# Two blocks on one core: the head of the first block with x transposed on the host, unscaled x for q, k, v and four gates, and idle TensorE products

## The reference, cut to what matters

```
xn   = rms_norm(x, mix_norm)                       # over the 1024 columns of a row
proj = xn @ w_in + b_in                            # 1024 x 4352
q, k, v, cb, cc, cx, ga, gc = split(proj)          # 512, 128, 128, 512, 512, 512, 1024, 1024
attn = sliding_window_attention(q, k, v, sinks)
conv = cb * causal_depthwise_conv(cc * cx, conv_w)
merged = sigmoid(ga) * (attn @ w_attn_branch) + sigmoid(gc) * (conv @ w_conv_branch)
h = x + merged @ w_out
```

## Time and profile before

| what | value |
|---|---|
| runs | 1231.47 us median of 3 (1231.33 to 1234.18) |
| the profiled execution's own time | 1231.15 us |
| its span, first to last instruction | 1229.4 us |
| TensorE products (PE) | 1206.5 us busy, 98%, 5844 instructions |
| TensorE weight loads (PEld) | 1013.6 us |
| VectorE (DVE), ScalarE (ACT), GpSimd (POOL) | 830.3, 554.4, 343.1 us |
| HBM read | 112.25 MB |

### The profile page before, as it was taken

How to read it: one execution, slowest core, us unless ns; L and a number is a source line. 1 busy time by engine, 2 the same in 40 slices (tenths; PEclk the granted TensorE clock), 3 DMA queues, 4 the chain that set the end, 5 groups by cost and what they waited for, 6 DMA issues and landing times.

```text
span 1229.4 us, 15053 instructions
## 1 busy us (share of the span) xinstructions
PE 1206.5 (98%) x5844; PEld 1013.6 (82%) x5844; DVE 830.3 (68%) x1532; ACT 554.4 (45%) x965; POOL 343.1 (28%) x267
## 2 busy tenths in 40 slices
PE   7999999999999999999999999999999999999997
PEld 6888888888888888888887789888788889888886
DVE  6788434436788536653568966778966766778964
ACT  6667332324444314433434456644335555553433
POOL 0255499972000000000003853343003033342000
PEclk9999999999999999999999999999999999999999
DMA  5322232223323322332323233222222332322221
GB/s 197 105 69 69 95 103 94 94 86 103 96 93 104 102 88 90 96 116 91 99 65 109 99 109 99 90 89 77 77 70 91 116 103 87 92 86 88 76 71 69
DMA packets 36152, 115.33 MB, mean 94 GB/s; under 512 B 3824, under 2 KB 6384, under 8 KB 36080
## 3 DMA queue, kind: packets, MB, share of 16 engines
q1 hardware_dynamic: 36080, 114.36, 29.3%
HBM read 112.25 MB, written 2.10 MB: 93 GB/s over the span
## 4 chain that ended last, share of the span: by engine, by line
PE 76%; DVE 14%; ACT 6%; issue 2%; POOL 1%; DMA 0%; SPq 0%; ACTq 0%
PE ps L273 73%; DVE RA L250 6%; DVE FA L250 4%; ACT RA L242 3%; DVE FA L262 2%; ACT FA L247 1%; ACT RA L246 1%; POOL FA L250 1%; DVE FA L1267 1%; PE ps L1301 1%; DVE RA L262 1%; DVE FA L1271 1%; PE ps L747 0%; DMA FA<-x 0%; ACT FA L246 0%
## 5 line engine op out<-in xcount | busy, mean ns | idle before, releaser
L273 PE MATMUL ps<-RA 128*128 128x512 f32 (+3 forms) x5460 | 1177.3, 376 | 7.1 <-DVE RA L250 4.8
L273 PEld LDWEIGHTS ps<-RA 128*128 128x128 f32 x5460 | 970.8, 188 | 191.1 <-DVE RA L250 4.9
L250 DVE TENSOR_TENSOR RA<-FA,RA 128x1024 fp32r<-128x1024 f32 (+4 forms) x316 | 329.3, 1051 | 185.6 <-ACT RA L242 183.6
L242 ACT ACTIVATE RA<-FA 128x1024 fp32r<-128x1024 f32 (+6 forms) x336 | 278.8, 858 | 334.7 <-PE ps L273 164.5
L250 POOL TENSOR_TENSOR FA<-FA 128x512 f32<-128x512 f32 (+1 forms) x89 | 122.1, 1372 | 550.5 <-ACT FA L246 451.5
L266 POOL TENSOR_SCALAR FA<-FA 128x256 f32<-128x256 f32 (+2 forms) x117 | 141.7, 1222 | 190.4 <-DVE FA L270 189.3
L262 DVE SCALAR_TENSOR_TENSOR FA<-ps,FA 128x512 f32<-128x512 f32 (+3 forms) x137 | 98.1, 721 | 95.6 <-PE ps L273 50.3
L247 ACT ACTIVATE FA<-FA 128x512 f32<-128x512 f32 (+3 forms) x113 | 61.0, 541 | 99.1 <-DVE FA L1271 78.4
L246 ACT ACTIVATE FA<-ps,FA 128x512 f32<-128x512 f32 x61 | 41.6, 685 | 123.5 <-PE ps L273 123.5
L262 DVE SCALAR_TENSOR_TENSOR FA<-FA 128x4 f32<-128x4 f32 (+4 forms) x166 | 81.8, 501 | 17.8 <-ACT FA L246 6.6
L250 DVE TENSOR_TENSOR RA<-ps,RA 128x256 fp32r<-128x256 f32 (+3 forms) x111 | 54.7, 529 | 21.4 <-ACT RA L246 18.9
(11 more groups left out here) (46 smaller groups left out, 305.8 us busy)
## 6 DMA issues: line engine op xcount, KB each, us to landing
FA<-w_units SPq DMA_DIRECT2D x190, 512.0 KB, 3.5
FA<-rel SPq DMA_DIRECT2D x16, 256.0 KB, 3.3
FA<-w_units SPq DMA_DIRECT2D x8, 384.0 KB, 3.0
FA<-x SPq DMA_DIRECT2D x4, 512.0 KB, 6.8
FA<-dmat SPq DMA_DIRECT2D x8, 256.0 KB, 3.2
out<-FA SPq DMA_DIRECT2D x8, 256.0 KB, 2.2
FA<-gain SPq DMA_DIRECT2D x1, 512.0 KB, 3.7
FA<-positions SPq DMA_DIRECT2D x1, 256.0 KB, 3.5
```

Of the source, the lines that this page charges most:

```text
L242: return lambda eng: eng.activation(dst, src, ACT.Copy)
L250: return lambda eng: eng.tensor_tensor(dst, a, b, op)
L273: return lambda e: e.matmul(dst, a, b, start=start, stop=stop_)
```

## The change

x comes twice from the host: transposed, as eight tiles of 128 x 512 (256 KB each), and by rows. The transposed tiles are loaded straight to where they are kept; the 32 transposes, the copies from PSUM and the loads in four pieces are gone. The row form is loaded in four pieces of 512 KB, only for the sums of squares; the first two stand behind all x tiles on SyncE's queue, the last two behind the fourth weight unit. The loads of `pvec` and `ident` move from SyncE's queue to ScalarE's. The first weight unit comes in two halves, and `gemm_first` runs its products in another order: for each half, four of high x high, four of high x low, four of low x high. Ahead of them stand ten products of a zeroed tile with itself, whose result nobody reads (`WARM`).

Unscaled x has a place of its own (X0H, X0L), so normalised x no longer overwrites it. The units k and v, and four gate units (ga0, gc0, ga1, gc1), which move up from the loop over the mixing units to here, run on unscaled x; VectorE multiplies their results by r, and the four gates' tanh then runs on SBUF. r is wanted later: its spread moves from the middle of q.w1 to the middle of q.w3, and the normalising of the eight tiles is spread over the evacuations of k, v and the four gates. The loop over the mixing units runs its six remaining gate pairs two ahead, with four buffers per gate; its last two turns have no gates.

```diff
+WARM = 10
...
-F_COLS = Y + 6760
-XIN, JUNK = Y, Y + 4096
+XIN = Y
+QT = Y + 256
+TG = Y + 6760
+F_COLS = TG + 2048
+X0H, X0L = Z + 16896, Z + 20992
...
+    for m in range(2):
+        u += [(f"ga{m}", tall("w_in", 2304 + 128 * m)), (f"gc{m}", tall("w_in", 3328 + 128 * m))]
     for t in range(4):
         u.append((f"cc{t}", tall("w_in", 1280 + 128 * t)))
         u.append((f"cx{t}", tall("w_in", 1792 + 128 * t)))
         u.append((f"cb{t}", tall("w_in", 768 + 128 * t)))
     for m in range(8):
-        u.append((f"ga{m}", tall("w_in", 2304 + 128 * m)))
-        u.append((f"gc{m}", tall("w_in", 3328 + 128 * m)))
+        if m < 6:
+            u.append((f"ga{m + 2}", tall("w_in", 2304 + 128 * (m + 2))))
+            u.append((f"gc{m + 2}", tall("w_in", 3328 + 128 * (m + 2))))
...
+        def gemm_first(key, banks, xh, xl):
+
+            h, l = w_slot[0]
+            for i in range(2):
+                halves = ((h, xh, [f"xh.{i}", f"wh.0.{i}"]), (h, xl, [f"xl.{i}"]), (l, xh, [f"wl.0.{i}"]))
+                for n, (w, xop, after) in enumerate(halves):
+                    for m, b in enumerate(banks):
+                        fin = f"gemm.{key}" if i == 1 and n == 2 and m == 3 else None
+                        T(fin, after if m == 0 else [], mmul(bank(b), R(w + 512 * i + 128 * m, 128), R(xop(i)),
+                                                             i == 0 and n == 0, False))
...
-        dma("ident", [], F(ID, 128), consts[0], "c0")
...
-
-            dma(f"x.{j}", [], steps(F(XIN + 256 * j, 256), [[1024, 4], [1, 256]]),
-                x_cols[:, :, 256 * j:256 * j + 256], f"x{j}")
...
-        load_x(0)
-        dma("pvec", [], F(PV, PV_COLS), pvec, "c1")
-        load_to(0)
-        load_x(1)
-        load_to(1)
+        def load_x(k):
+
+            dma(f"x.{k}", [], F(H + 512 * k), x[k], f"x{k}")
+
+        def load_half(i):
+
+            dma(f"raw.0.{i}", [], F(RAW + 512 * i), w_units[0][:, 512 * i:512 * i + 512], f"rawfirst{i}")
+
+        def load_rows(t):
+
+            dma(f"rows.{t}", [], F(XIN + 1024 * t, 1024), x_rows[128 * t:128 * t + 128], f"rows{t}")
+
+        dma("pvec", [], F(PV, PV_COLS), pvec, "c1", "scalar")
+        dma("ident", [], F(ID, 128), consts[0], "c0", "scalar")
+        for i in range(2):
+            load_x(i)
+            load_half(i)
+        issued[0] = 1
         load_x(2)
         load_x(3)
+        load_to(1)
+        load_x(4)
+        load_x(5)
         load_to(2)
+        load_x(6)
+        load_x(7)
+        for t in range(2):
+            load_rows(t)
         HB, NSINK, SS, MS, RC, TMP = columns(16), columns(8), columns(4), columns(4), columns(4), columns(4)
-        SQ = columns(8)
...
-        def turn_x(k):
-            for t in range(4):
-                b = xt_bank(k)
-                T(f"xT.{k}" if t == 3 else None, [f"x.{k // 2}", "ident"] + take(f"bank{b}") if t == 0 else [],
-                  lambda e, t=t, b=b: e.transpose(bank(b, 128, 128 * t), F(XIN + 1024 * t + 128 * k, 128), F(ID, 128)))
+        x0h = lambda k: X0H + 512 * k
+        x0l = lambda k: X0L + 512 * k
+
+        for n in range(WARM):
+            T(None, ["z1a"] if n == 0 else [], mmul(bank(7), R(K2A, 128), R(K2A), True, True))
...
-            b, gain = xt_bank(k), F(PV + PV_G1 + k, 1)
-            A(f"xh.{k}", [f"xT.{k}", "pvec"], func(R(xh(k)), bank(b), ACT.Copy, scale=gain))
-            yield
-            V(f"xl.{k}", [f"xh.{k}"], stt(R(xl(k)), bank(b), gain, Rf(xh(k)), ALU.mult, ALU.subtract))
...
-        def keep_x(k):
-            b = xt_bank(k)
-            (V if k < 4 else A)(f"h0.{k}", [f"xl.{k}"], (lambda e: e.tensor_copy(F(H + 512 * k), bank(b))) if k < 4 else copy(F(H + 512 * k), bank(b)))
-            free(f"bank{b}", f"h0.{k}")
...
-        def square_x(half):
-            for t in range(4):
-                A(f"ss.{half}.{t}", [f"x.{2 * half}", f"x.{2 * half + 1}"] + [f"ss.0.{t}"] * half, func(
-                    F(JUNK + 512 * t, 512), F(XIN + 1024 * t + 512 * half, 512), ACT.Square, accum=F(SQ + 4 * half + t, 1)))
...
-        for k in range(4):
-            turn_x(k)
-        staggered(first_operand(k) for k in range(2))
-        prepare_to(0)
-        staggered(first_operand(k) for k in range(2, 4))
-        for k in range(4):
-            keep_x(k)
-        square_x(0)
+            gain = F(PV + PV_G1 + k, 1)
+            A(f"xh.{k}", [f"x.{k}", "pvec"], func(R(x0h(k)), F(H + 512 * k), ACT.Copy, scale=gain))
+            V(f"xl.{k}", [f"xh.{k}"], stt(R(x0l(k)), F(H + 512 * k), gain, Rf(x0h(k)), ALU.mult, ALU.subtract))
+
+        def square_rows(t):
+
+            A(f"ss.{t}", [f"rows.{t}"], func(F(XIN + 1024 * t, 1024), F(XIN + 1024 * t, 1024), ACT.Square, accum=F(SS + t, 1)))
+
+        for i in range(2):
+            first_operand(i)
+            A(f"wh.0.{i}", [f"raw.0.{i}"], copy(R(WH + 512 * i), F(RAW + 512 * i)))
+            V(f"wl.0.{i}", [f"wh.0.{i}"], sub(R(WL + 512 * i), F(RAW + 512 * i), Rf(WH + 512 * i)))
+        Q.at["wl.0"] = Q.at["wl.0.1"]
+        prepared[0] = 1
+        load_to(3)
+        for t in range(2, 4):
+            load_rows(t)
+        first_operand(2)
+        first_operand(3)
+        prepare_to(1)
+        first_operand(4)
+        first_operand(5)
+        prepare_to(2)
+        first_operand(6)
+        first_operand(7)
...
-        for g in range(4):
-            gemm_wide(f"q.w{g}", [2 * g, 2 * g + 1], qb, xh, xl, g == 0, g == 3, lambda k: [f"xl.{k}"])
-            if g == 0:
-                for k in range(4, 8):
-                    turn_x(k)
-                square_x(1)
-                V("ss", ["ss.0.3", "ss.1.3"], add(F(SS, 4), F(SQ, 4), F(SQ + 4, 4)))
-                bit_rstd("rc", SS, MS, RC, TMP, ["ss"], 1.0 / 1024, 1e-5, V)
-                staggered(first_operand(k) for k in range(4, 8))
-                keep_x(4)
-
-                def spread_rstd():
-                    spread("rb", RC, 0, ["rc"])
-                    A("rn", ["rb"], copy(F(RB), bank(0)))
-                    free("bank0", "rn")
-
...
+        def spread_rstd():
+            spread("rb", RC, 0, ["rc"])
+            A("rn", ["rb"], copy(F(RB), bank(0)))
+            free("bank0", "rn")
+
+        def normal(k):
+            return normalise("x0", k, PV + PV_G1, "rn", "rn", (V, G)[k % 2])
+
+        def scaled(key, b, dst, room):
+
+            V(f"{key}.n", [f"gemm.{key}", "rn"] + room, mul(F(dst), bank(b), F(RB)))
+            free(f"bank{b}", f"{key}.n")
+
+        def q_scale(m):
+            V(f"qn.{m}", ["gemm.q.w3", "rn", "ss.3"], mul(F(QT + 512 * m), bank(qb[m]), F(RB)))
+            free(f"bank{qb[m]}", f"qn.{m}")
+
...
+            yield from stacked_q(f"q{m}", qb[m], QA + 512 * m, QB + 512 * m, [f"qn.{m}"], bin_ + m, src=(QT + 512 * m, f"qt{m}"))
+
+        def k_evacuate():
+            t, tn = t_slot()
+            scaled("k", 5, t, take(tn))
+            yield from stacked_k("k", 5, K1A, K1B, K2A, K2B, ["k.n"], "z1", bin_ + 4, src=(t, tn))
+
...
+            t, tn = t_slot()
+            scaled("v", 6, t, take(tn))
+            A("vf", ["v.n"], func(F(VF), F(t), ACT.Identity, bias=F(bin_ + 5, 1)))
+            free(tn, "vf")
+            yield
+
...
+        def early_gate(w, m, b, c, col):
+            gemm_tall(f"{w}{m}", b, x0h, x0l)
+
+            def evacuate():
+                scaled(f"{w}{m}", b, c, [])
+                yield
+                A(f"{w}t.{m}", [f"{w}{m}.n"], func(F(c), F(c), ACT.Tanh, scale=0.5, bias=F(HB + col + m, 1)))
+            return evacuate()
+
+        gemm_first("q.w0", qb, x0h, x0l)
+        square_rows(0)
+        square_rows(1)
+        prepare_to(3)
+        square_rows(2)
+        square_rows(3)
+        bit_rstd("rc", SS, MS, RC, TMP, ["ss.3"], 1.0 / 1024, 1e-5, V)
+        for g in range(1, 4):
+            if g == 3:
                 midway.append(spread_rstd)
-            if g == 1:
-                for k in range(5, 8):
-                    keep_x(k)
-            staggered(normalise("x0", k, PV + PV_G1, "rn", f"gemm.q.w{k // 2}", (V, G)[k % 2]) for k in NORMALISED[g])
-        dma("mask", ["ss.1.3", "xT.7"], F(MASK, 256), consts[1:3].rearrange("a p q -> p a q"), "c2")
-        gemm_tall("k", 5, xh, xl, 8, lambda k: [f"x0.l{k}"])
-
-        def q_evacuate(m):
-            t, tn = t_slot()
-            V(f"qn.{m}", ["gemm.q.w3"] + take(tn), mul(F(t), bank(qb[m]), F(RB)))
-            free(f"bank{qb[m]}", f"qn.{m}")
-            yield from stacked_q(f"q{m}", qb[m], QA + 512 * m, QB + 512 * m, [f"qn.{m}"], bin_ + m, src=(t, tn))
-
-        k_split = stacked_k("k", 5, K1A, K1B, K2A, K2B, ["gemm.k"], "z1", bin_ + 4)
-        staggered([q_evacuate(0), q_evacuate(1), k_split, q_evacuate(2), q_evacuate(3)])
-        gemm_tall("v", 6, xh, xl)
-        A("vf", ["gemm.v"], func(F(VF), bank(6), ACT.Identity, bias=F(bin_ + 5, 1)))
-        free("bank6", "vf")
+            gemm_wide(f"q.w{g}", [2 * g, 2 * g + 1], qb, x0h, x0l, False, g == 3, lambda k: [f"xl.{k}"])
```

(39 more changed lines are left out.)

29 lines of the change are left out of this document (14 added, 15 removed).

## The result

The changed kernel took **1226.68 us** (median of four runs, 1225.61 to 1226.96) against 1232.22 for the kernel before in the same session (four runs, 1231.33 to 1234.18): ratio 0.995, 95% interval 0.9938 to 0.9962. That is 5.5 us, 0.45%, faster; the steps of the prediction summed to 7.3. The profiled execution of the changed kernel took 1226.96 us with a span of 1225.2, so between the two profiled executions the gain is 1231.15 - 1226.96 = 4.2 us.

The account below looks back on a forecast made before the run. TensorE bounds the kernel, busy 1206.5 of 1229.4 us. Terms 4.6 + 0.5 + 1.7 + 0.9 + 0.2 - 0.6 = 7.3 take 1231.15 to 1223.9, with the median's 0.3 1224.2 us; range 1221.5 to 1229.

Parts of the forecast that it names:

- First product earlier: Head: with x arriving transposed, the first dense product starts at 5.9 instead of 10.51; gain 4.6 us.
- the sum of issue times: Head: moving the pvec and ident loads off SyncE's queue saves 0.44 us of issue and no more.
- Slow start: q.w0: idle products raise the clock before the first dense products; 0 to 1.1 us left, middle taken, gain 0.5.
- Transposes: Head: all 32 go; the 16 behind q.w0 give 1.66 us, the others are inside the first term.
- is its weight there?: Start of q.w1 at 11.9: raw.1 lands at 9.5 and is ready at 11.8, just in time.
- the loads set the head: Rival, head: raw.1 and raw.2 come 3 to 4 us late, gain only 3.3, 1228.2 us; chance 0.12.
- Root-mean-square: Spread in q.w3: r ready at 24.2, wanted at 25.6; gain 0.9 us with 1.4 us of cover.
- the slower rival: q.w3: rows of x arrive too late, the spread stops TensorE; 1237 us at 200 GB/s; chance 0.05.
- Gates moved: Early gates to cc0: VectorE's added scalings leave thin slack; 0.6 us charged as lost, bounds 0 and 4.1.
- the chain as forecast: x's last normalised tile, behind gc1's scaling at 62.0: ready at 66.5, wanted by cc0 at 66.6.
- early gates starve on VectorE: Rival, gates to cc0: GpSimd's low parts hold VectorE's scalings; loss 4.1 instead of 0.6, 1227.7 us; chance 0.14.
- The step that failed: Behind V's bias, from 53.17 in the kernel before: TensorE is dense, so the rest shifts as a block.

Follow-up runs that it names:

- Experiment 5: Changed kernel with the pvec and ident loads back on SyncE's queue ahead of x; 1226.82 us, ratio 0.9957.
- experiment 3: Changed kernel plus eight idle products in TensorE's wait ahead of the transposes of the squares, near 670 us; 1225.53 us, ratio 0.9944.
- Experiment 1: Changed kernel without its ten idle products (WARM = 0); 1227.41 us, ratio 0.9958.
- experiment 6: Kernel before plus ten idle products at its head, x still by rows and turned; 1232.17 us, ratio 0.9997.
- experiment 7: Changed kernel with the four early gates put back in the loop over the mixing units; 1239.59 us, ratio 1.0059.
- Experiment 2: Changed kernel with x's last tile normalised ahead of gc1's scaling in VectorE's queue; 1225.66 us, ratio 0.9944.
- experiment 9: The changed kernel run once more, unaltered; 1226.78 us, ratio 0.995.
- experiment 4: Kernel before plus eight idle products in its wait ahead of the squares, at 674.2 us; 1232.73 us, ratio 1.0001.
- experiment 8: Changed kernel with tile reorder, idle products before the squares, raw.1 ahead of x.2 and x.3, earlier split of output units' weights; 1223.67 us, ratio 0.9931.
- experiment 11: Repeat in the last session of the kernel of experiment 8; 1223.75 us, ratio 0.9929.
- the fill: Eight idle products in TensorE's wait ahead of the squares; added alone to the changed kernel 1225.53 us, to the kernel before 1232.73 us.
- the best version: The four-edit kernel of experiment 8, repeated in experiment 11; 1223.67 and 1223.75 us, ratios 0.9931 and 0.9929.
- the edit to the first weights: raw.1's load and rounding moved ahead of x.2 and x.3, against the changed kernel; part of the best version, 1223.67 us.

## Why the prediction was right

The direction, the size within its range (1224.2 forecast, 1226.68 measured, range 1221.5 to 1229), and the reason for most of it held: TensorE's idle time at the head was the place, and data and queues moved there as worked out. By its own steps:

- **First product earlier:** 5.72 instead of 10.51, 4.8 gained, 4.6 forecast. The first weight half landed at 4.72 (5.2 forecast) and was rounded just before the idle products ended. The last of them held TensorE until 5.72 and not 5.5, so the idle products cost the start 0.2 us. Experiment 5 bears out the sum of issue times.
- **Slow start:** q.w0's 24 products took 5.75 us (5.72 to 11.47) where before had 6.69, so 0.9 instead of the middle value 0.5. Here luck has a part: in experiment 3, whose head is the same, three dense products still came 0.43 us apart and took the 0.5 us back. Experiment 1 takes the idle products away and gets the slow products back. What the prediction left open, whether x's new layout was needed for it, experiment 6 answers: without early data they are worth nothing.
- **Transposes** and **is its weight there?** The prediction said that the two gains above don't add, since raw.1's low part would be ready at 11.8; it was ready at 11.67 and q.w1 started at 11.81 (11.9 forecast). 4.8 + 0.9 + 1.7 would be 7.4, and q.w1 came 6.9 earlier: the wait for raw.1 took most of the rest (0.34 us of idle time). Here the rival "the loads set the head" was right in kind: the wait for raw.1 was 0.34 us here, and none, 0.71, 0.86 and 1.32 in four other executions with the same head (experiments 3, 7, 2 and 9). That is at most 1.3 of the 3 to 4 us that the rival asked.
- **Root-mean-square:** the spread came at 25.53 (25.6 forecast) without a wait, so the rows of x came in time and the slower rival fell.
- **Gates moved:** here a term was mis-sized. It charged 0.6 and gave both ends, 0 and 4.1. The low weights of the last early gate were done at 54.7 (54 forecast) and cost nothing. The place was right, x's last tile ahead of cc0, and the size was 1.62. In the chain as forecast gc1's scaling came at 62.0, as soon as its products were done; it came at 63.73, since on VectorE cx0's low weights and tile 6 stand ahead of it, and the weights waited for ScalarE. The chain as forecast left these two out. GpSimd's last step gave 0.5 back (1.26 us instead of 1.8). Experiment 2 shows that the order on VectorE made the wait, and experiment 7 that the gates are worth far more than they cost. The rival "early gates starve on VectorE" named this tile, but gave GpSimd's low parts as the reason. Of the four only the first held VectorE (at 35.15 us a low half of q took 1.78 us instead of 0.74), and TensorE had no wait from it; during the other three VectorE was idle.

VectorE beside GpSimd cost more outside the stretch that the prediction walked through. Rows of the changed kernel's timeline, 255 to 262 us, GpSimd, VectorE (two narrow windows, as the two rows are of different widths) and TensorE's weight loads:

```profile
255.00 3.00 POOL L257 TENSOR_TENSOR FA<-FA 128x512 f32<-128x512 f32 x2
255.02 1.83 DVE L257 TENSOR_TENSOR RA<-FA,RA 128x512 fp32r<-128x512 f32 x1 [0.70 <-ACT RA L249]
256.77 2.31 DVE L257 TENSOR_TENSOR RA<-FA,RA 128x1024 fp32r<-128x1024 f32 x1
...
259.13 3.04 PEld L280 LDWEIGHTS ps<-RA 128*128 128x128 f32 x14 [0.57 <-DVE RA L257]
```

Two low parts, one of a merged tile and one of a weight unit, run beside GpSimd's two-input steps and take 1.83 and 2.31 us, where parts of these widths alone took 0.69 and 1.23 (the rows at 64.51 and 61.92 above). TensorE waits for the second. Some 0.4 of the 0.6 us lost between 68 and 662 us lie here: in the executions of experiments 1 and 2, which lack this wait, that stretch is 593.5 us long instead of 593.9. The Trainium skill, SBUF — State Buffer, section SBUF: two separate sides, has VectorE operations with two SBUF inputs and GpSimd operations that read SBUF exclude each other; the trace agrees, 1.83 us instead of 0.69 and 2.31 instead of 1.23.

**The step that failed** stands at the end of the first part: "Behind that TensorE is dense, so I take the rest of the kernel to shift as a block." The waits did shift as a block (1.85 us ahead of the squares in both). The clock didn't: in the profiled execution the same wait was followed by a fall that cost 1.6 us, which no term held. Experiments 6 and 9 show that it comes and goes in either kernel, so whether a profiled execution has it is luck, as far as these runs show; that filling the wait prevents it is suggested by experiments 3, 4, 8 and 11 and not shown. Whether the changed kernel has it more often than before stays open. The sum of the profiled pair closes with these three: 7.3 forecast, less 1.0 at cc0 (1.62 for 0.6), 0.6 on the way and 1.6 by the fall make 4.1, and 4.2 were measured.

With the order, the fill and the first weights mended, the best version gains 8.9 to 9.4 us on before by the medians. Set against the profiled execution of before, as the sum is, its two profiled executions gain 7.8 and 7.4 us (1223.39 and 1223.75 against 1231.15), the sum's 7.3; the edit to the first weights, which the sum did not hold, is in that.

Open: why the first weights land up to 1.2 us apart between executions of one kernel; what the fill is worth by itself; whether splitting the output units' weights earlier matters by itself (it was run only with the other edits, and the executions of experiments 1 and 2, without it, had no wait there either); and where the longer runs of the best version (1225.14, 1225.25 and 1225.81, all with a mean granted clock of 0.997) have their fall.

## What to carry to other kernels

When the bound engine is dense, moving its start earlier moves every producer's deadline with it: before looking for the next gain at the head, walk each queue to the first operand that must now come earlier (here x's normalised tiles), and look first at the order within that queue, since one exchange gave back 1.0 us. Idle products that lift the clock paid here only where real work followed them without a wait. And a short wait in the middle can cost more than its length, where the clock falls behind it (1.4 to 1.7 us here); a few products of no use in that wait are worth trying, over enough runs to tell them from what else varies.
